# A sixth seven-product down chunk in three SwiGLU stages, with kept banks copied by ScalarE and summed by accumulating transfers

## The reference

```
x += 1/2 * SwiGLU_a(rms(x))
x += Mixer_l(rms(x))            # retention|Mamba-2, or sparse|sliding-window attention
x += CrossAttn(rms(x), rms(mem))
x += 1/2 * SwiGLU_b(rms(x))
swiglu(h, w_gate, w_up, w_down) = (silu(h @ w_gate) * (h @ w_up)) @ w_down   # D 1024, D_FF 2816
```

## Time and profile before

| | us |
|---|---|
| median of 3 timed runs | 1182.55 |
| lowest, highest | 1182.21, 1182.57 |
| profiled execution, device time | 1182.64 |
| its span | 1180.7 |
| PE busy | 1173.8 (99%) |
| PE weight loads busy | 1025.7 (87%) |
| DVE busy | 944.4 (80%) |
| ACT busy | 688.1 (58%) |
| POOL busy | 105.0 (9%) |
| DMA, q1 (the loads), share of 16 engines | 56.2% |

### The profile page before, as it was taken

How to read it: one execution, slowest core, us unless ns; L and a number is a source line. 1 busy time by engine, 2 the same in 40 slices (tenths; PEclk the granted TensorE clock), 3 DMA queues, 4 the chain that set the end, 5 groups by cost and what they waited for, 6 DMA issues and landing times.

```text
span 1180.7 us, 17445 instructions
## 1 busy us (share of the span) xinstructions
PE 1173.8 (99%) x6787; PEld 1025.7 (87%) x6787; DVE 944.4 (80%) x1102; ACT 688.1 (58%) x925; POOL 105.0 (9%) x97
## 2 busy tenths in 40 slices
PE   9999999999999999999999999999999999999998
PEld 8888889889989888888888888889887898888886
DVE  6687897875657689888978988997887676798887
ACT  7566556853557566555565655564576556565553
POOL 1010001420142010000010000010012121000000
PEclk9999999999999999999999999999999999999999
DMA  9966755454344465665655656547623435666561
GB/s 319 334 205 197 204 188 179 144 182 141 141 145 176 143 197 162 212 212 181 202 189 177 208 185 205 185 143 214 212 92 127 144 114 166 203 217 198 191 195 55
DMA packets 164013, 214.93 MB, mean 182 GB/s; under 512 B 14832, under 2 KB 139120, under 8 KB 163824
## 3 DMA queue, kind: packets, MB, share of 16 engines
q1 hardware_dynamic: 163664, 213.30, 56.2%
q0 software_dynamic: 144, 0.52, 0.1%
q10 hardware_dynamic: 144, 0.26, 0.1%
HBM read 213.02 MB, written 1.05 MB: 181 GB/s over the span
## 4 chain that ended last, share of the span: by engine, by line
PE 98%; DMA 1%; ACT 0%; POOL 0%; DVE 0%; SPq 0%; issue 0%; POOLq 0%; DVEq 0%
PE ps L2302 30%; PE ps L2309 16%; PE ps L2281 15%; PE ps L2282 15%; PE ps L2283 15%; PE ps L2385 1%; PE ps L2572 1%; PE ps L3036 1%; PE ps L2892 1%; DMA arena<-in_first 1%; PE ps L3059 0%; PE ps L2580 0%; PE ps L2997 0%; PE ps L2994 0%; PE ps L2453 0%; PE ps L2644 0%
## 5 line engine op out<-in xcount | busy, mean ns | idle before, releaser
L2302 PE MATMUL ps<-hT,w_parts 128*128 128x512 f32 x1568 | 375.4, 391 | 0.3 <-issue 0.2
L2302 PEld LDWEIGHTS ps<-hT,w_parts 128*128 128x128 f32 x1568 | 289.8, 188 | 59.6 <-issue 1.5
L1355 DVE TENSOR_TENSOR w_parts<-raw,w_parts 128x2048 fp32r<-128x2048 f32 x85 | 196.2, 2317 | 58.0 <-ACT w_parts L749 57.9
L2309 PEld LDWEIGHTS ps<-hT,w_parts 128*128 128x128 f32 x1568 | 201.4, 191 | 8.0 <-DVE w_parts L1431 0.2
L884 ACT ACTIVATE w_parts<-raw 128x2048 fp32r<-128x2048 f32 x108 | 206.1, 1908 | 0.6 <-DMA raw<-in_ffn_w_gate 0.6
L749 ACT ACTIVATE w_parts<-raw 128x2048 fp32r<-128x2048 f32 x85 | 162.4, 1920 | 73.5 <-PE ps L2283 70.5
L2309 PE MATMUL ps<-hT,w_parts 128*128 128x256 f32 x1568 | 204.1, 283 | 0.0
L1571 DVE TENSOR_TENSOR w_parts<-raw,w_parts 128x2048 fp32r<-128x2048 f32 x45 | 103.0, 2289 | 14.3 <-ACT w_parts L884 14.3
L2281 PE MATMUL ps<-w_parts,arena_r 128*128 128x512 f32 (+1 forms) x264 | 102.8, 389 | 0.0
L2282 PE MATMUL ps<-w_parts,arena_r 128*128 128x512 f32 (+1 forms) x264 | 102.8, 389 | 0.0
L2283 PE MATMUL ps<-w_parts,arena_r 128*128 128x512 f32 (+1 forms) x264 | 102.3, 387 | 0.0
(11 more groups left out here) (373 smaller groups left out, 1975.1 us busy)
## 6 DMA issues: line engine op xcount, KB each, us to landing
raw<-in_ffn_w_down SPq DMA_DIRECT2D x44, 1024.0 KB, 5.0
raw<-in_ffn_w_gate SPq DMA_DIRECT2D x43, 1024.0 KB, 5.4
raw<-in_ffn_w_up SPq DMA_DIRECT2D x43, 1024.0 KB, 5.4
raw<-in_xattn_wkv SPq DMA_DIRECT2D x16, 1024.0 KB, 5.4
raw<-in_even_w_in SPq DMA_DIRECT2D x13, 1024.0 KB, 5.2
raw<-in_xattn_wq SPq DMA_DIRECT2D x8, 1024.0 KB, 5.1
raw<-in_xattn_wo SPq DMA_DIRECT2D x8, 1024.0 KB, 5.4
raw<-in_odd_w_in SPq DMA_DIRECT2D x6, 1024.0 KB, 5.6
```

What stands on the lines that cost most here:

```text
L1355: ins = V.tensor_tensor(lo, src, hi.bitcast(F32), ALU.subtract)
L2302: mm(ps[:, bank0 + m, :], cols(w_hi, n, k, CW, m * P, (m + 1) * P), hT[:, k, :, :].rearrange("p a c -> p (a c)"), start=k == 0, stop=False)
L2309: last = mm(ps[:, bank0 + m, SEQ:], cols(w_lo, n, k, CW, m * P, (m + 1) * P), hT[:, k, 0, :], start=False, stop=k == KT - 1)
```

## The change

Stages 1 to 3 get six mixed chunks instead of five: down chunks 1, 2, 4, 5, 7 and 8. The loops become one of three turns, run twice (mixed, mixed, plain). DVE no longer adds banks 0 to 3 to kept. ACT copies them: for the first mixed chunk into kept, for each later one into two buffers `copied` in `arena` (half 0 and half 1). POOL then issues an accumulating transfer from `copied` onto kept, one for each half, so ten in each of the three stages, of 512 KB each. ACT's next copy into a buffer waits for the transfer that read it, and each transfer for the one before it on its half. DVE's first two `kept_sum` move behind the last gate_scale, where it first waits for the last two transfers. Stage 0 keeps its work; some semaphores are merged (`pool_set`).

```diff
         class Mixed:
-            FIRST, COUNT = (2, 0, 0, 0), (3, 5, 5, 5)
+            FIRST, COUNT = (2, 0, 0, 0), (3, 6, 6, 6)
...
-            kept = [[part(at_, [2, 512]) for at_ in (10240, 4992)], kept_later, kept_later, kept_later]
+            copied = [part(at_, [2, 512]) for at_ in (10240, 4992)]
+            kept = [copied, kept_later, kept_later, kept_later]
...
+        def kept_added_at(f, i):
+
+            return ((f - 1) * (Mixed.COUNT[f] - 1) + i - 1) * 16
...
-                    if first_out is not None:
-                        act.wait_ge(mixed_mm[f], mixed_mm_at(f, first_out) + 1)
-                        nc.scalar.activation(Mixed.kept[f][0], ps[:, 0:2, :], ACT.Copy).then_inc(mixed_read[f], 1)
+                    if out is not None:
+                        act.wait_ge(mixed_mm[f], mixed_mm_at(f, out) + 1)
+                        if added and (f > 1 or not isinstance(out, int) or out > 1):
+                            act.wait_ge(kept_added_in[0], kept_added_at(f, out))
+                        nc.scalar.activation((Mixed.copied if added else Mixed.kept[f])[0], ps[:, 0:2, :],
+                                             ACT.Copy).then_inc(mixed_read[f], 1)
...
-                    turn(2, mixed=1, first_out=0)
-                    turn(3)
-                    with act.Fori(2, mixed_end(f)) as i:
-                        turn(i * 2, mixed=i)
-                        turn(i * 2 + 1)
+                    turn(2, mixed=1, out=0)
+                    turn(3, out=1, added=True)
+                    with act.Fori(1, 3) as g:
+                        turn(g * 3 + 1, mixed=g * 2)
+                        turn(g * 3 + 2, mixed=g * 2 + 1, out=g * 2, added=True)
+                        turn(g * 3 + 3, out=g * 2 + 1, added=True)
...
-                    turn_read(3, 1)
-                    with dve.Fori(2, mixed_end(f)) as i:
-                        turn_mixed(i * 2, i)
-                        turn_read(i * 2 + 1, i)
+                    turn(3)
+                    with dve.Fori(1, 3) as g:
+                        turn_mixed(g * 3 + 1, g * 2)
+                        turn_mixed_next(g * 3 + 2, g * 2 + 1)
+                        turn(g * 3 + 3)
                 made[0] = base + FFN_CHUNKS - 1
-                kept_sum(0, 2, 0)
-                kept_sum(1, 3, 2)
+                if f == 0:
+                    kept_sum(0, 2, 0)
+                    kept_sum(1, 3, 2)
                 gate_sum(FJ - 1)
                 gate_scale(FJ - 1)
+                if f:
+                    for half in range(2):
+                        dve.wait_ge(kept_added_in[half], kept_added_at(f, mixed_end(f)))
+                    kept_sum(0, 2, 0)
+                    kept_sum(1, 3, 2)
                 kept_sum(2, 2, 1)
                 kept_sum(3, 1, 3)
...
+            def ffn(f):
+
+                for i in range(1, Mixed.COUNT[f]):
+                    for half in range(2):
+                        pool.wait_ge(mixed_read[f], mixed_read_at(f, i) + half + 1)
+                        if f > 1 or i > 1:
+                            pool.wait_ge(kept_added_in[half], kept_added_at(f, i))
+                        pool.dma_start(Mixed.kept[f][half], Mixed.copied[half],
+                                       accum_op=ALU.add).then_inc(kept_added_in[half], 16)
...
-                with pe.Fori(2, mixed_end(f)) as i:
-                    turn(i * 2, False, kept=i)
-                    turn(i * 2 + 1, False, mixed=i)
+                if f:
+                    with pe.Fori(1, 3) as g:
+                        turn(g * 3 + 1, False, kept=g * 2)
+                        turn(g * 3 + 2, False, mixed=g * 2)
+                        turn(g * 3 + 3, False, kept=g * 2 + 1, mixed=g * 2 + 1)
```

More of the change, by code:

```diff
@@ L510, in build @@
         mixed_read = [quarter_in[0]] + [es["kz_done"]] * 3
+        kept_added_in = [sem(f"kept_added_in{half}") for half in range(2)]
+        def kept_added_at(f, i):
+            return ((f - 1) * (Mixed.COUNT[f] - 1) + i - 1) * 16
         def mixed_end(f):
@@ L877, in hidden, with turn @@
                                          ACT.Copy).then_inc(gu_hi_done, 1)
-                def turn(j, between=lambda c: None, mixed=None, first_out=None):
+                def turn(j, between=lambda c: None, mixed=None, out=None, added=False):
                     def split(m):
@@ L906, in turn @@
                     hidden(j + (f * FJ + 1), gu_hi)
[L907 to L909 removed]
+                    if out is not None:
+                        if added and (f > 1 or not isinstance(out, int) or out > 1):
+                            act.wait_ge(kept_added_in[1], kept_added_at(f, out))
+                        nc.scalar.activation((Mixed.copied if added else Mixed.kept[f])[1], ps[:, 2:4, :],
+                                             ACT.Copy).then_inc(mixed_read[f], 1)
+                    if mixed is not None and out is not None:
                         sums_hi()
@@ L945, in ffn @@
                          mixed=2)
-                    turn(5, first_out=2)
+                    turn(5, out=2)
                     turn(6, mixed=3)
@@ L2271, in _ @@
                                     ALU.mult).then_inc(os_["c2_read"], 1)
+                for f in range(1, 4):
+                    if v == norm_no(f // 2, 3 * (f % 2)):
+                        ffn(f)
             last_norm()
```

32 lines of the change are left out of this document (16 added, 16 removed).

## The result

| | median, us | lowest to highest | ratio to before, 95% interval |
|---|---|---|---|
| before (4 runs beside it) | 1182.43 | 1182.21 to 1182.57 | |
| changed | 1212.18 | 1211.14 to 1214.08 | 1.0254 (1.0236 to 1.0271) |

The changed kernel is 29.8 us slower. The forecast was 1184.7 us with a range up to 1194.0: the sign of the likeliest case was right, its size was off by a factor of fourteen, and the time lies outside the range. The profiled execution took 1214.08 us, its span is 1212.3 us.

What follows compares the result with a forecast made beforehand. PE, holding 98% of what ended last, was taken as the bound. The sum 1182.64 - 2.04 - 0.87 + 1.75 + 3.3 gave 1184.8 us, 1184.7 against the median; range 1180.3 to 1194 us.

Steps and rivals of the forecast that it cites:

- the likeliest case: Last transfers of each stage land 6.2 to 9 us after issue and stop DVE, then PE: 1182.2 to 1190 us, 45%.
- PE's saving: One chunk in each of three stages turns from plain to mixed, three matmuls fewer each: -2.04 us.
- the small wait that goes: Turns 3, 6 and 9: PE's 0.29 us delay at the gate after the mixed chunk disappears, -0.87 us over three stages.
- DVE's order: Stage ends: all four kept_sum behind gate_scale make the last hidden chunk 1.41 us later; PE waits, +1.75 us in all.
- A second 1.34 us of each engine for the addition: Estimate that an accumulating transfer, reading the destination too, takes another 1.34 us of each DMA engine: 6.5 us alone, 8.1 crowded.
- X: Last transfer's time from issue to landing at a stage's end: 7.3 us in stages 1 and 2, 6.5 in stage 3; +3.3 us.
- the upper bound: Last transfer at each stage end: 8.1 us crowded plus a 2.1 us wait, 10.2 us; stops of 12.9 us over three stages.
- the rival in time: Last transfers land in under 5.95 us everywhere, so DVE does not wait for them: 1181.4 us, 30%.
- Load slots: New transfers share DMA engines with weight loads inside the loop; late loads taken as 0, up to 3 us in the range.
- the 1.46 us of room: In the loop, DVE ends down chunk 2's low part at 470.76; PE starts on it at 472.22, 1.46 us later.
- The slow rival: Additions at a quarter of a copy's rate; half 1 lands about 11.9 us after its copy: 18 us of stops, 1199 us, 12%.
- late loads by themselves: Crowding makes DVE's split late in turns 4 and 7: up to 3 us, 1187 to 1188 us, 5%.

## Why the prediction was wrong

**Right, by the runs.** PE's saving, the small wait that goes and DVE's order: 1181.4 forecast, 1181.77 measured without transfers. The order by itself 2.2 us for 1.75. The small wait: in the changed kernel the gate of turn 3 starts 4.79 us behind the start of the mixed chunk (471.98, 476.77), where it was 4.93. ACT's copies and their waits cost nothing. The direction of the likeliest case. A second 1.34 us of each engine for the addition, called an estimate: 2.7 us in all in the trace. In stage 3, with no load beside it from 1184 us on, the last transfer took 6.7 us from issue to DVE (1182.45 to 1189.17) and DVE stood idle 0.93 us, where the sum had X = 6.5 and 0.55. No issue was held by DVE: the thirty took 0.86 to 0.94 us, the first 1.06, with an operation of DVE beside or without one, so the 2.1 us of the upper bound were not there. Nor did the transfers land in the 4.4 us worked out for the rival in time; their median was 6.5 us.

**Wrong: "Load slots", taken as 0, with up to 3 us in the range.** It is 15.0 us by the account and 16.3 to 17.5 by the delayed transfers (which shorten other waits a little too), the largest term. The step looked at one load that landed 1.6 us late and excused it with another load beside it. It never asked how full the DMA engines are in that stretch. The DMA view of the kernel before, 476 to 492 us, would have told:

```profile
q1 hardware_dynamic: 3153, 3.97, 76.9%
```

Two transfers of 2.7 us make 34% more, 111% in all. So everything in the stretch lands late, the loads by up to 3.6 us, and not by the 1.6 us that the one row had shown. The down chunk is needed at once: DVE is idle 4.32 us at its sums in turn 4 and 3.52 us in turn 7, and what is left of that behind the 1.46 us of room reaches PE.

**Wrong: X in stages 1 and 2, 7.3 us.** It was 11.1, and DVE stood idle 5.4 and 5.3 us, not 1.36. The stops sum to 11.8 us for 3.3 and lie near the upper bound of 12.9 that the prediction had worked out. The step took the middle of "alone" and "crowded" where half 0, half 1 and two loads of 1 MB were all under way. The DMA view of the changed kernel, 570 to 592 us, shows these loads (from 580 to 590 us the engines' share is 1.03):

```profile
raw<-in_xattn_wkv SPq DMA_DIRECT2D x1, 1024.0 KB, 9.4
raw<-in_ffn_w_gate SPq DMA_DIRECT2D x1, 1024.0 KB, 9.7
```

The slow rival named 11.9 us for this landing, from an addition at a quarter of the rate; the landing was nearly that, the reason another: two transfers and the loads share full engines.

**Missed: the clock behind a stop.** 5.6 us by the account, 2.2 us a stop in the kernel with a stop and nothing else. The prediction passed a stop on one for one. The chain of waits that it read had PE busy all the time, so no row showed what a stop does to the price of the matmuls behind it.

**The chances.** The slow rival had 12%, late loads by themselves 5%, and both were taken as alternatives. They are two losses at two places of a stage, but full DMA engines stand behind both, and they came together; the range of the sum should have let them. Of the signs named for them, the gap of 5 us at `kept_sum` and PE idle before mixed chunks were seen, and ACT waiting at its copies for a transfer was not.

## What to carry to other kernels

Before a transfer is added to a loop, add up the DMA engines' busy share in the stretch where it would stand, not over the run: the run's 56% hid 77% here. A sum just under 100% is no safety either, for the plain transfers brought it to 94% and cost 13 us. A transfer that nobody waits for soon belongs in the stretch behind the load that somebody does wait for; one wait at its issue was worth 17 us. And a stop of TensorE can cost more than its length: the five stops of 5.6 to 6.7 us cost 1.7 to 2.2 us more each in slower matmuls, and of those of 2.0 to 3.0 us most, not all, were followed by the lower clock.

## What the runs showed of the hardware

An accumulating transfer from SBUF to SBUF takes twice the DMA engines' time of a plain one, 2.7 against 1.33 us of each engine for 512 KB. With nothing but two such transfers under way (1184 to 1188 us, end of stage 3) the engines are full at 187 GB/s; loads alone reach 329 GB/s at 99.2% in the kernel without transfers (476 to 482 us).

```profile
DMA packets 214, 0.75 MB, mean 187 GB/s; under 512 B 31, under 2 KB 31, under 8 KB 214
q0 software_dynamic: 214, 0.75, 95.2%
```

(The Trainium skill, Collectives: The Full Stack, "The bandwidth ceiling: the fold count and why AG ≠ RS ≠ AR", says that an addition in a DMA engine reads two sources and so runs at half the rate of a copy, for transfers between cores. The trace agrees for SBUF to SBUF on one core.)

GpSimd's addition of 128x1024 takes 2.5 to 3.4 us and lengthens DVE's SBUF-only operations beside it, by 2.1 and 2.2 us in the two shown. A stop is followed by the lower clock not in every case: behind the 1.99 us of stage 3 in the changed kernel it was 0.70 over 5 us; behind the 3.00 us of stage 1 in the kernel with plain transfers it stayed at 1.00, behind the 2.20 us of stage 2 it was 0.75; and of the five stops of 2.47 us in the kernel with all additions on DVE two were followed by 1.00. What decides that between 2 and 3 us these runs leave open.
